# A gated linear recurrence layer: its four projections as three F32R passes instead of one F32 product, and the value projection turned afterwards

## The reference, cut to what matters

```
q, f, i, gate = split(h @ w_in, 4)             # 1024 -> 4 x 1024
g = log(lb + (1 - lb) * sigmoid(f))            # log decay
k = (1 - lb) * sigmoid(-f)
q = silu(q) / sqrt(128)
# per head (8 heads of 128), v = i, in chunks of the sequence:
o_t = q_t . S_t,   S_t = exp(g_t) * S_(t-1) + k_t v_t^T
x = x + (rmsnorm(o) * silu(gate)) @ w_out
```

## Time and profile before

| | |
|---|---|
| median of three runs | 2713.71 us (2711.9 to 2714.17) |
| the profiled execution's own time | 2717.71 us |
| its span in the trace | 2715.9 us |
| TensorE busy | 2393.9 us, 88% of the span |
| TensorE weight loads busy | 1878.4 us |
| VectorE, ScalarE, GpSimd busy | 1198.1, 1062.2, 780.3 us |
| mean granted clock of TensorE | 0.935 of full |

### The profile page before, as it was taken

The page is one execution under the profiler, slowest core; times in us unless marked ns, Lnnn a source line. Parts: engine busy times, 40 slices in busy tenths (PEclk is TensorE's granted clock), DMA queues, the critical chain, the costliest instruction groups (busy, mean ns, idle before and its releaser), DMA issues. The chain is left out here.

```text
span 2715.9 us, 47687 instructions
## 1 busy us (share of the span) xinstructions
PE 2393.9 (88%) x17830; PEld 1878.4 (69%) x17830; DVE 1198.1 (44%) x1912; ACT 1062.2 (39%) x1807; POOL 780.3 (29%) x834
## 2 busy tenths in 40 slices
PE   2998999999859999999995867995969989999996
PEld 2965666666746777767774767995969656666656
DVE  3123555655323335554356233665141335555552
ACT  3045544544212332333323314665130644544431
POOL 4234322322311122222122332553322433323211
PEclk8999999999879999999995888997989989999998
DMA  2110433433211110011100101111111214334332
GB/s 95 63 42 16 125 102 106 117 101 93 94 47 40 41 49 23 36 48 49 41 18 10 56 6 55 53 35 34 31 39 55 104 40 121 108 100 118 108 127 94
DMA packets 101394, 179.13 MB, mean 66 GB/s; under 512 B 15402, under 2 KB 84012, under 8 KB 99524
## 3 DMA queue, kind: packets, MB, share of 16 engines
q1 hardware_dynamic: 101188, 176.36, 21.1%
HBM read 160.61 MB, written 15.70 MB: 65 GB/s over the span
## 5 line engine op out<-in xcount | busy, mean ns | idle before, releaser
L1818 PE MATMUL ps<-normed,w_slots 128*128 128x344 f32 x1152 | 366.9, 476 | 27.0 <-DMA w_slots<-in_w_hgrn 26.8
L1171 POOL TENSOR_TENSOR latents_t_lo<-pages_t,latents_t_hi 128x256 fp32r<-128x256 f32 x256 | 187.0, 731 | 556.9 <-ACT latents_t_hi L1386 556.2
L1818 PEld LDWEIGHTS ps<-normed,w_slots 128*128 128x128 f32 x1152 | 225.7, 200 | 144.4 <-issue 45.7
L367 PE MATMUL ps<-src_hi,w_hi 128*128 128x344 f32 x1008 | 219.1, 327 | 104.5 <-POOL w_lo L338 104.5
L1528 DVE TENSOR_REDUCE sums<-w_uq 128x8 f32<-128x512 f32 x256 | 175.2, 684 | 271.6 <-ACT w_uq L1394 271.1
L367 PEld LDWEIGHTS ps<-src_hi,w_hi 128*128 128x128 f32 x1008 | 173.6, 193 | 107.4 <-POOL w_lo L338 107.4
L1248 PE MATMUL ps<-w_uk_hi,latents_t_hi 128*128 128x512 f32 x512 | 236.4, 462 | 0.0
L1394 ACT ACTIVATE w_uq<-ps 128x512 f32<-128x512 f32 x256 | 152.8, 597 | 213.3 <-PE ps L1248 212.5
L338 POOL TENSOR_TENSOR w_lo<-w_slots,w_hi 128x1024 fp32r<-128x1024 f32 (+1 forms) x50 | 104.7, 2093 | 413.1 <-ACT w_hi L307 413.1
L367 PE MATMUL ps<-src_lo,w_hi 128*128 128x344 f32 x1008 | 217.3, 324 | 0.0
L367 PE MATMUL ps<-src_hi,w_lo 128*128 128x344 f32 x1008 | 215.8, 323 | 0.0
(11 more groups left out here) (294 smaller groups left out, 4551.5 us busy)
## 6 DMA issues: line engine op xcount, KB each, us to landing
pages_t<-in_pages_t SPq DMA_DIRECT2D x256, 208.0 KB, 2.6
pages<-in_pages SPq DMA_DIRECT2D x256, 128.0 KB, 2.1
w_slots<-in_w_hgrn SPq DMA_DIRECT2D x32, 512.0 KB, 4.1
w_slots<-in_w_mla_in SPq DMA_DIRECT2D x18, 512.0 KB, 3.5
w_slots<-in_w_rg SPq DMA_DIRECT2D x16, 512.0 KB, 3.6
residual<-in_x SPq DMA_DIRECT2D x4, 1032.0 KB, 6.9
residual<-in_x SPq DMA_DIRECT2D x1, 4128.0 KB, 14.3
x_home<-residual SPq DMA_DIRECT2D x1, 4128.0 KB, 15.5
```

What stands on the lines that cost most here:

```text
L367: mm = nc.tensor.matmul(c.ps[:, NT * u + t, 0:TT], a[:, u, k, :], b[:, k, cols], start=(k == 0 and n == 0), stop=(k == kt - 1 and n == 2))
L1171: nc.gpsimd.tensor_tensor(lat_lo[:, g % DEPTH, :, :].rearrange("p k t -> p (k t)"), ring[:, g % RING, 0:KVL], lat_hi[:, g % DEPTH, :, :].r ...
L1818: mm = nc.tensor.matmul(bank[:, 0:TT], ws[:, kind, kk, :], c.h[:, kk, t * TT:(t + 1) * TT], start=(kk == 0), stop=(kk == KD - 1))
```

## The change

The four kinds are projected as features by tokens in three F32R passes: high weight by high `h`, high weight by low `h`, low weight by high `h`. The parts of `h` are made once (8 copies on ACT, 8 subtractions on DVE). The parts of each weight block are made on the way: `weight_hi` on ACT and `weight_lo` on POOL, four each for a head, in two slots instead of four. The values i are made with features on the partitions like the others, and a new kind of unit, TURN, transposes them by three tiles on TensorE, from where ACT copies them to `v`. A head now has 15 units. Their order is f, q, i (9 units), then g0, TURN0, g1, TURN1, g2, TURN2.

To make room, `raw`, `differences` and `factors` take the place of `c.h`, and `heads_out` the place of `c.x`. The residual is written to memory (`x_home`) at the start and read back slice by slice in the output projection. The loop over heads is unrolled differently: heads 0, 5, 6 and 7 are written out and 1 to 4 are a loop of two passes.

```
-    NU = 12
+    UNITS = [(kind, t) for kind in range(3) for t in range(NT)] + \
+            [unit for t in range(NT) for unit in ((3, t), (TURN, t))]
+    NU = len(UNITS)
+    LAST_UNIT = [UNITS.index((kind, NT - 1)) + 1 for kind in range(4)]
...
-        ws = st.sb("w_slots", [P, 4, KD, P])
-        raw = st.sb("raw", [P, 3, T])
+        ws = st.sb("w_slots", [P, 2, KD, P])
+        w_hi = st.sb("w_hi", [P, 2, KD, P], F32R)
+        w_lo = st.sb("w_lo", [P, 2, KD, P], F32R)
+        h_hi = st.sb("normed_hi", [P, KD, T], F32R)
+        h_lo = st.sb("normed_lo", [P, KD, T], F32R)
+        raw = c.h[:, 0:4, :]
...
+        dd = c.h[:, 4:6, :]
+        z = c.h[:, 6:8, :]
...  # SP, one head
+                sp.dma_start(sin[:, :, :], dram["state_hgrn"]...)
+                if following is not None:
+                    weights(following, 2, lo_before[2])
+                    weights(following, 3, lo_before[3])
+                sp.wait_ge(ns_done, ns_now)
+                sp.dma_start(dram["o_hgrn_s"]..., ns[:, :, :])
+                if after is not None:
+                    weights(after, 0, lo_before[0])
+                    weights(after, 1, lo_before[1])
+                sp.wait_ge(state_done, states_now)
+                sp.dma_start(dram["o_hgrn_p"]..., states[:, CHUNKS - 1, :])
...  # SP, start
+            weights(0, 0)
+            weights(0, 1)
             sp.dma_start(att[:, :, :], dram["hgrn_masks"]).then_inc(loads, 16)
...
+            weights(0, 2)
+            weights(0, 3)
+            sp.dma_start(dram["x_home"], c.x[:, :, :]).then_inc(spilled, 16)
+            weights(1, 0)
+            weights(1, 1)
...  # TensorE
+                bank = c.ps[:, 4 + (n + u) % 2, :]
                 wait(pe, unit_drained, NU * h + (n - 1))
+                if kind == TURN:
+                    for tt in range(3 * t, 3 * t + 3):
+                        rows = P if tt < QT else NS
+                        mm = nc.tensor.transpose(bank[0:rows, tt % 3 * P:(tt % 3 + 1) * P],
+                                                 raw[:, 3, tt * P:tt * P + rows], c.ident[:, :])
...
+                    pe.wait_ge(w_lo_done, 4 * h + (kind + 1))
+                for kk in range(KD):
+                    for m, (w, x) in enumerate(((w_hi, h_hi), (w_hi, h_lo), (w_lo, h_hi))):
+                        mm = nc.tensor.matmul(bank[:, 0:TT], w[:, slot, kk, :], x[:, kk, cols],
...
-                fill(2)          # behind line 1898
+                fill(4)
...
-                fill()           # behind lines 1905, 1907
+                fill(2)
...  # ACT
                 level_exp(h, 0)
+                if following is not None and not (isinstance(h, int) and h == 0):
+                    weight_hi(following, 1)
...
                     fill(1 if l else 2)
+                    if following is not None and l in (1, 4):
+                        weight_hi(following, 2 if l == 1 else 3)
...
-                fill(3)
+                fill(1)
+                if after is not None:
+                    weight_hi(after, 0)
+                fill(4)
...
-                    fill()           # behind the silu of q
+                    fill(2)
...  # POOL, behind line 2029
+                if following is not None and not (isinstance(h, int) and h == 0):
+                    weight_lo(following, 1)
...  # POOL, behind line 2045
+                    if following is not None and l in (2, 5):
+                        weight_lo(following, 2 if l == 2 else 3)
...  # POOL, behind line 2050
+                if after is not None:
+                    weight_lo(after, 0)
...  # hgrn_layer
-        out = st.sb("heads_out", [P, KD, T])
+        out = c.x
...
+        output_projection(c, c.dram["w_hgrn_out"], KD, out, following(layer), x_in=c.dram["x_home"])
...  # streamed_projection, SP
+            def x_blocks(lo, hi):
+                for k in range(lo, hi):
+                    sp.wait_ge(src_lo_done, k + 1)
+                    sp.dma_start(c.x[:, k, :], x_in[:, k, :]).then_inc(x_landed[k // 2], 16)
...
-    nc = bacc.Bacc("TRN2", target_bir_lowering=False, num_devices=1)
+    nc = bacc.Bacc("TRN2", target_bir_lowering=False, num_devices=1,
+                   dynamic_dma_scratch_size=1024)
```

More of the change, by code:

```diff
@@ L282, in streamed_projection @@
         drained = st.sem("block_drained")
+        x_landed = [st.sem(f"x_landed{n}") for n in range(KD // 2)] if x_in is not None else []
         norm = None if norm_layer is None else Norm(c, st, norm_layer)
@@ L393, in _ @@
                 dve.wait_ge(x_back, 16)
-            with dve.Fori(0, pairs) as i:
+            for n, landed in enumerate(x_landed):
+                dve.wait_ge(landed, 32)
                 for u in range(2):
-                    one(2 * i + u, u)
+                    one(2 * n + u, u)
+            if x_in is None:
+                with dve.Fori(0, pairs) as i:
+                    for u in range(2):
+                        one(2 * i + u, u)
             if blocks % 2:
@@ L1624, with heads @@
 KINDS = ("f", "q", "i", "g")
[L1627 to L1633, removed]
+TURN = len(KINDS)
+def heads(engine, head):
+    head(0, 0, 1, 2)
+    with engine.Fori(0, 2) as i:
+        head(2 * i + 1, 1, 2 * i + 2, 2 * i + 3)
+        head(2 * i + 2, 0, 2 * i + 3, 2 * i + 4)
+    head(H - 3, 1, H - 2, H - 1)
+    head(H - 2, 0, H - 1, None)
+    head(H - 1, 1, None, None)
 def hgrn_lower_bound(c, layer, lb, olb):
@@ L1773, in _ @@
             sp.dma_start(gn[:, :], dram["hgrn_g_norm"]).then_inc(loads, 16)
[L1775 to L1803, removed]
+            weights(0, 2)
[3 more added lines that the diff above has]
+            weights(1, 1)
+            heads(sp, head)
             sp.wait_ge(ns_out, 16 * H)
@@ L1969, in log_decay, with head @@
                 nc.scalar.activation(gl[:, 0:SEQ], sg[:, 0:SEQ], ACT.Ln).then_inc(ln_done, 1)
-            def head(h, u, following):
+            def head(h, u, following, after):
                 units = iter(range(NU) if following is not None else [])
@@ L2015, in head @@
                 nc.scalar.activation(rs, rs, ACT.Exp, scale=-0.5).then_inc(rs_done, 1)
+            for kk in range(KD):
+                nc.scalar.activation(h_hi[:, kk, :], c.h[:, kk, :], ACT.Copy).then_inc(h_hi_done, 1)
+                if kk == 1:
+                    weight_hi(0, 0)
+            weight_hi(0, 1)
             for n in range(NU):
                 drain_unit(0, 0, n)
+                if n + 1 in LAST_UNIT:
+                    kind = LAST_UNIT.index(n + 1) + 2
+                    weight_hi(kind // 4, kind % 4)
             forget_key_query(0)
@@ L2021, in _, with weight_lo, head @@
             log_decay(0)
-            heads_in_pairs(act, head)
+            heads(act, head)
         @block.gpsimd
         def _(pool):
-            def head(h, u, following):
+            def weight_lo(h, kind):
+                slot = kind % 2
+                pool.wait_ge(w_hi_done, 4 * h + (kind + 1))
+                nc.gpsimd.tensor_tensor(w_lo[:, slot, :, :], ws[:, slot, :, :], w_hi[:, slot, :, :].bitcast(F32),
+                                        ALU.subtract).then_inc(w_lo_done, 1)
+            def head(h, u, following, after):
                 pool.wait_ge(sin_landed, 16 * h + 16)
@@ L2051, in head @@
                   .then_inc(zp_done, 1)
-            heads_in_pairs(pool, head)
+                if after is not None:
+                    weight_lo(after, 0)
+            for n in range(6):
+                weight_lo(n // 4, n % 4)
+            heads(pool, head)
         @block.vector
```

104 lines of the change are left out of this document (64 added, 40 removed).

## The result

The changed kernel takes 2694.4 us (2693.2 to 2696.01, four runs) against 2712.99 us (2711.9 to 2714.17) for the kernel before on the same chip. The ratio is 0.9932, with a 95% interval of 0.9915 to 0.9949. That is 18.6 us faster, where 50 us were forecast, and 0.4 us above the upper end of the forecast's wider range, 2694 us. Its profiled execution has a span of 2691.4 us, 24.5 us less than before; the profiled execution of the kernel before was 4 us slower than its median.

A forecast was written before the change was run, and what follows sets the result against it. TensorE was taken to bound the kernel except in the passage between heads. Steady heads 39, head 0 8.5, start 3.3, last head -0.5 sum to 50.3 us saved: 2663 us median; main range 2639 to 2686, 8 in 10 2632 to 2694.

The forecast's parts named there:

- the passage between heads: From the output sums to level 1 (26.7 us), other engines' chain sets the time; shorter units win nothing there.
- the third point on the chain: q's weight split on ACT and POOL ahead of level 0: +1.5 us there, +0.7 at level 1, +0.2 at level 2.
- Rival 2: Weight splits enter the chain, POOL's and ACT's queues holding back every level; 2698 us if half enters; chance 0.12.
- The clock: More idle time in the passage between heads lets TensorE's clock fall; 0.8 us a head, bounds 0 and 3.8.
- rival 3: TensorE falls to half clock in the levels too; with four slow units a head 2772 us, slower; chance 0.06.
- the wait ahead of u0: TensorE waits 2.3 us for ACT's copy of g2 before the following head's first unit; no cost in the chain.
- The scans: Sample state loaded ahead of the weights, so its scaling leaves DVE's scans: 3.91 to 2.63 us, -1.3 a head.
- the unit's price: A TensorE unit takes 3.79 us in three F32R passes, against 4.63 for f, q, g and 5.58 for i.
- level 2 to the output sums: Rest of a steady head, where TensorE sets the pace: 7.5 us shorter than 51.7, so 44.2 us.
- the residual's way through memory: Write at the start (15.5 us) and read back in the output projection, both covered: nothing; some 15 us if uncovered.
- The 1.0 us at level 3: Loss in each steady head: `weight_lo` of kind i stands ahead of POOL's level 3 product and waits for `weight_hi`.
- The last head: The head without units of a following head has a longer ACT chain: 0.5 us lost.

The follow-up runs named there:

- e11: The changed kernel with one more unit of the following head ahead of level 0 and all later units a place up, q's split unmoved; 2667.6 us.
- e5: On e4, one more unit of the following head issued ahead of level 0, all later units a place up; 2629.4 us.
- e1: The changed kernel with GpSimd's low part of q's weights cut to 8 of 1024 columns in heads 1 to 6; 2683.4 us.
- e2: The changed kernel with GpSimd's whole subtraction for q's low weights moved behind its product for level 1; 2665.6 us.
- e10: On e4, ACT copies the last g unit ahead of the table load for q, not behind q's silu; 2659.8 us.
- e3: The changed kernel with q's high weight part made earlier on ACT, right behind the copy of the last g unit; 2674.7 us.
- e7: The kernel before with only the sample state's load issued ahead of the weight loads; 2712.8 us against 2714.1.
- e6: On e4, SP issues the sample state's load behind the two weight loads, as the kernel before did; 2675.0 us.
- e8: On e4, GpSimd makes the low part of i's weights behind its product for level 3, not ahead of it; 2658.1 us.
- e9: On e5, the low part of i's weights moved behind GpSimd's product for level 3, as in e8; 2620.3 us.
- e4: The changed kernel with both parts of q's weights made by DVE in its pause between k and the scans, none on ACT or GpSimd; 2660.3 us.

## Why the prediction was wrong

The direction was right and so was the reading that the passage between heads is the other engines' chain, where shorter units win nothing. e11 shows it, and e5.

**The step that failed** is the third point on the chain: q's `weight_hi` and `weight_lo` at the top of a head, taken as +1.5 us at level 0, +0.7 at level 1 and +0.2 at level 2. Level 0 came 2.2 us later than in rows 5, but level 1 4.3 us and level 2 5.3 us. I treated it as a delay that fades. The delay itself I had too large: GpSimd's product for level 0 came 2.4 us later (23.2 us behind the output sums against 20.8) and not 3.5. What I had far too small was DVE's slowing down beside it, 9.9 us for work of 4.8; the 5.1 us more, less the 0.8 by which it started earlier, are the 4.3 us at level 1. The traces show a chain of exclusions: `w_lo` holds DVE for 2.1 us (e1), and GpSimd's product for level 0, late behind the wait for ACT's `w_hi` in the queue, lands on DVE's product, and so on down to level 1, for 3.0 us more (e1 against e2). Rival 2 named the mechanism, and gave it 2698 us for entering half; its chance was 0.12 and should have been much nearer to the main case. Its place was not every level, as it said, but the one passage that the forecast itself had found to be without slack.

**The clock** had 0.8 us a head. The unit between level 1 and level 2 took 5.5 us and not 3.79. From level 1 to level 2 it was 6.3 to 6.8 us in the six heads, where e10 at full clock has 5.0. The unit of half clock was taken to be covered by the chain ahead of level 0; it stood behind level 1, where nothing covers it. The longer passage alone is not the reason: in e3 level 1 comes at 26.8 us, and level 2 some 7.0 us behind it in five of six heads. The kernel before had such a stretch too, in two of six heads (7.1 and 7.9 us against 5.5), and the rows of the forecast came from one that did not. What decides when the clock falls in this passage is open. The Trainium skill, "TensorE: Matmul & The Clock Gate", section HAM oscillation, says that pauses between groups of products bring the half clock back. The windows at 0.82 and, with the pause filled, 0.94 agree. But rival 3's price by it for the wait ahead of u0, 3.8 us in each head, is not what the runs show: without the wait a head is 0.6 us shorter (e10).

**The scans** were a term of -1.3 us read from one head. They do take 2.63 us in each head afterwards. But line 2080 takes 24.0 us over the eight heads of the kernel before, 3.0 us each and not 3.91, so -0.4 us. e7 found no gain in the kernel before. In e6, in a shorter passage, the same load order costs 14.7 us.

**Right:** the unit's price (3.79 us; from 1029.6 to 1033.4 us in the trace), level 2 to the output sums (44.6 against 44.2 us), head 0 (8.8 against 8.5 us), the start (4.1 against 3.3), and the residual's way through memory, which costs nothing that is seen: from the first product of the output projection to its last sum it is 93.8 us, and 92.8 before, 1 us in which I have no cause. The wait ahead of u0 was there, 2.5 us, and nearly free (e10: at most 0.6 us a head). The 1.0 us at level 3 was there too, 1.1 us, and shown to be `weight_lo` of kind i by e8 and e9. The last head came 1.0 us shorter (62.95 us), where 0.5 us longer was forecast; it lies between 62.6 and 64.3 us in the other runs, and why is open.

Sum for a steady head: 6.5 forecast, less 3.6 (level 1 at 31.0 us and not at 26.7 + 0.7 = 27.4), less 0.7 (from there to level 2 6.5 us and not 5.0, with 0.8 allowed for the clock), less 0.4 (44.6 us behind level 2 and not 44.2) gives the 1.8 measured.

With q's split out of the way (e4) the kernel took 2660.3 us, and 2663 had been forecast. That is partly luck: level 1 came 1.5 us earlier than forecast there, and the stretch behind it was slower.

## What to carry to other kernels

Where a stretch is found to be a chain without slack, price each instruction put near it at its full length and ask what it shares with the chain's engine: here GpSimd's and VectorE's two-input work excluded each other, and the place of one subtraction was worth 29 us of 2694. Read a term that is to be multiplied by the heads from all of them; one head had the scans at 3.91 us, their mean was 3.0. And a pause in TensorE is a place for a unit: moving one there gained 27 us in the changed kernel (e11) and 31 us in e4 (e5), more than the new arithmetic did in its first form. In e5 it also kept the slow stretch behind level 1 away, and a further edit then gained 9 us that had gained 2 before.

## What the hardware showed that was not expected

VectorE's rounding copy of 128x1024 takes 0.69 us alone and 2.39 us when GpSimd's scaling has started shortly ahead of it (e6 and e4), although this copy reads only one tensor. It ends 0.6 us after the scaling has ended, so these two take turns as well. VectorE's timeline of e6, then of e4, then GpSimd's of e4:

```profile
1072.82 0.69 DVE L2163 CAST w_hi<-w_slots 128x1024 fp32r<-128x1024 f32 x1
```
```profile
1068.14 2.39 DVE L2163 CAST w_hi<-w_slots 128x1024 fp32r<-128x1024 f32 x1
1070.56 1.23 DVE L2165 TENSOR_TENSOR w_lo<-w_slots,w_hi 128x1024 fp32r<-128x1024 f32 x1
```
```profile
1067.52 2.46 POOL L2097 TENSOR_TENSOR sample_in<-sample_in,decay 128x1024 f32<-128x1024 f32 x1 [15.46 <-DVE decay L2133]
```

The same edit (i's subtraction behind level 3) gained 2.2 us in one order of units and 9.1 us in another, while it removed TensorE's wait at level 3 in both. What differed is the stretch from level 1 to level 2: 5.0 to 7.3 us in e4, 4.6 to 5.0 in e5.
